# ScalarE's gate exponential and logarithm placed ahead of the four output-gate copies, in both layers of the second block

## The reference, cut to what matters

```
aq, ak, av, az, mq, mk, mv, mo, mz, mi, mf = project(xn, w_in)
q = rope_2d(aq); k = rope_2d(ak)
att_x = window_ctx_attention(q, k, v, kc, vc, sink) * silu(az)
...
lf = log_sigmoid(mf + b_f)        # per token and head, 2 directions
b  = cumsum(lf)                   # within chunks of 128 tokens
```

## Time and profile before

| | |
|---|---|
| median of three runs | 2201.64 us (2199.36 to 2202.74) |
| profiled execution: own time | 2193.12 us |
| profiled execution: span | 2191.3 us |
| mean granted TensorE clock | 0.98 |
| PE busy | 2060.9 us, 94% of the span |
| DVE busy | 775.5 us, 35% |
| ACT busy | 404.6 us, 18% |
| chain that ended last | PE 88%, DMA 4%, DVE 4%, ACT 2% |

### The profile page before, as it was taken

How to read it: one execution, slowest core, us unless ns; L and a number is a source line. 1 busy time by engine, 2 the same in 40 slices (tenths; PEclk the granted TensorE clock), 3 DMA queues, 4 the chain that set the end, 5 groups by cost and what they waited for, 6 DMA issues and landing times.

```text
span 2191.3 us, 36820 instructions
## 1 busy us (share of the span) xinstructions
PE 2060.9 (94%) x15880; PEld 1489.7 (68%) x15880; DVE 775.5 (35%) x1750; ACT 404.6 (18%) x958; POOL 5.8 (0%) x12
## 2 busy tenths in 40 slices
PE   7999999999989999999999999999999989899877
PEld 6869999886866666666666655567545675466766
DVE  5735655586231121111011111013256364235354
ACT  1232210104220111000100000002133422123221
POOL 0000000000000000000000000000000000000000
PEclk9979999999999999999999999999999999999998
DMA  8473444336189999999999999991211101222100
GB/s 306 172 247 119 171 176 173 135 136 248 39 328 370 420 418 417 420 421 420 420 419 420 421 420 418 418 416 81 97 57 39 40 38 58 76 98 77 58 20 19
DMA packets 71939, 506.73 MB, mean 231 GB/s; under 512 B 7776, under 2 KB 9824, under 8 KB 11232
## 3 DMA queue, kind: packets, MB, share of 16 engines
q1 hardware_dynamic: 69296, 497.18, 56.8%
q0 software_dynamic: 1152, 4.19, 0.8%
q10 hardware_dynamic: 1328, 2.97, 0.4%
HBM read 503.27 MB, written 1.05 MB: 230 GB/s over the span
## 4 chain that ended last, share of the span: by engine, by line
PE 88%; DMA 4%; DVE 4%; ACT 2%; issue 1%; SPq 0%; DVEq 0%; ACTq 0%
PE ps L449 86%; DMA work<-weights 2%; DMA ring<-weights 2%; PE ps L1114 1%; PE ps L690 1%; PE ps L566 0%; DVE work L2527 0%; DMA par<-params 0%; DVE work L1885 0%; ACT work L1707 0%; DVE work L2484 0%; DVE work L2488 0%; DVE work L2485 0%; DVE work L2594 0%; PE ps L1215 0%
## 5 line engine op out<-in xcount | busy, mean ns | idle before, releaser
L449 PE MATMUL ps<-work 128*32 128x256 f32 (+8 forms) x5608 | 596.0, 385 | 30.5 <-DVE work L2527 11.3
L449 PE MATMUL ps<-work,ring 128*128 128x256 f32 (+2 forms) x2056 | 524.1, 410 | 12.0 <-DVE work L2409 6.0
L449 PEld LDWEIGHTS ps<-work 128*32 128x32 f32 (+3 forms) x5608 | 382.9, 139 | 196.6 <-issue 122.4
L449 PE MATMUL ps<-ring,work 128*32 128x256 f32 (+3 forms) x4824 | 471.9, 413 | 13.0 <-DMA ring<-weights 3.9
L449 PEld LDWEIGHTS ps<-work,ring 128*128 128x128 f32 x2056 | 356.2, 193 | 151.8 <-issue 115.8
L449 PEld LDWEIGHTS ps<-ring,work 128*32 128x32 f32 (+1 forms) x4824 | 260.2, 120 | 150.8 <-issue 80.0
L449 PE MATMUL ps<-xc,ring 128*128 128x256 f32 (+1 forms) x1440 | 277.2, 354 | 11.1 <-DVE xc L1901 7.1
L449 PEld LDWEIGHTS ps<-xc,ring 128*128 128x128 f32 x1440 | 244.6, 193 | 45.2 <-issue 12.1
L2147 DVE TENSOR_TENSOR work<-work,ps 128x256 f32<-128x256 f32 x42 | 17.7, 421 | 419.4 <-ACT work L1564 419.4
L449 PE MATMUL ps<-xc,work 128*128 128x256 f32 (+1 forms) x720 | 138.3, 350 | 0.3 <-DMA work<-weights 0.3
L449 PEld LDWEIGHTS ps<-xc,work 128*128 128x128 f32 x720 | 120.8, 191 | 20.2 <-issue 3.8
(11 more groups left out here) (266 smaller groups left out, 1163.1 us busy)
## 6 DMA issues: line engine op xcount, KB each, us to landing
ring<-weights SPq DMA_DIRECT2D x317, 1024.0 KB, 12.0
work<-weights SPq DMA_DIRECT2D x154, 1024.0 KB, 16.0
work<-rel POOLq DMA_DIRECT2D x8, 512.0 KB, 11.1
con<-consts ACTq DMA_DIRECT2D x1, 1368.0 KB, 10.3
xc<-x_t SPq DMA_DIRECT2D x1, 1024.0 KB, 7.4
xc<-ctx_t ACTq DMA_DIRECT2D x1, 1024.0 KB, 21.5
out<-work SPq DMA_DIRECT2D x1, 1024.0 KB, 3.9
par<-params SPq DMA_DIRECT2D x1, 872.0 KB, 9.2
```

Source lines behind the costliest of these rows:

```text
L449: ins = eng.matmul(o, lhs, rhs, start=start, stop=stop, **kw)
```

## The change

In ScalarE's `block2_first` the wait for `lf_abs`, the exponential, the wait between the two, and the logarithm move from behind the four `Silu` copies of `az` to ahead of them. It holds for both layers. No instruction is added or removed and no other engine's program changes.

```
@@ -1647,13 +1647,13 @@
                     else:
                         n = 2 * T if l else T
                         eng.activation(ak[:, 0:n], o[:, 0:n], ACT.Copy).then_inc(s["aqk_copied"], 1)
-                for c in range(CC):
-                    o = tile(eng, "az", l, c)
-                    eng.activation(azs[:, c, 0:n_q], o[:, 0:n_q], ACT.Silu).then_inc(s["azs_out"], 1)
                 eng.wait_ge(s["lf_abs"], l + 1)
                 eng.activation(labs, labs, ACT.Exp, scale=-1.0).then_inc(s["lf_ln"], 1)
                 eng.wait_ge(s["lf_ln"], 2 * l + 1)
                 eng.activation(labs, labs, ACT.Ln, bias=con[:, CN("one")]).then_inc(s["lf_ln"], 1)
+                for c in range(CC):
+                    o = tile(eng, "az", l, c)
+                    eng.activation(azs[:, c, 0:n_q], o[:, 0:n_q], ACT.Silu).then_inc(s["azs_out"], 1)
```

## The result

The changed kernel has a median of 2180.73 us (2172.15 to 2183.27) against 2200.86 us (2199.36 to 2202.74) of the kernel before, four executions each: ratio 0.9908, 95% interval 0.9881 to 0.9934. That is 20.1 us less, where 12.4 us were forecast, and the time lies under the range of 2185 to 2196 us. The profiled execution took 2172.15 us with a span of 2170.3 us, 21.0 us less than the one of before.

A forecast was written before the change was run, and what follows sets the result against it. PE, busy 94% of the span, was taken to bound the kernel. Wait 8.11 plus clock 4.35 gave 12.46 us, less 0.1 for hand-offs 12.4, so 2201.64 - 12.4 = 2189.2 us, range 2185 to 2196.

The forecast's parts named there:

- Step 1, cover: ACT ahead of the `az` copies: loads, `Exp` and `Ln` are covered by PE's `az` matmuls, 1.1 us margin in layer 1, cost 0.
- Step 2, subtraction: DVE's subtraction behind `rope`: `lf` is ready some 9 us before PE's last `az` matmul ends in layer 1.
- Step 3, the wait: PE between `az` 3 and the prefix sums: idle goes, 4.16 + 3.95 = 8.11 us gained, residual 0 or a few hundredths.
- Step 4, table loads: ACT's table loads in each layer: four before and four after, the last ahead of the same instruction, cost 0.
- Step 5, the clock: PE from the prefix sums to the second scores: clock no longer falls, 2.77 us in layer 0, 1.58 in layer 1, together 4.35.
- Step 6, what is late next: DVE and ACT from first scores to first probabilities: still in time for PE, 0.6 us left in layer 0, 4 more in layer 1.
- The seams together: Both layers, from the end of `az` to the second scores: 8.11 us of wait plus 4.35 of clock, 12.46 us gained.
- The rival of the wait alone: Only the wait goes; the clock still falls there, or later losses eat its gain: 8.1 us gained, 2193.5 us, chance 0.23.
- the rival of one layer: Layer 1 gains nothing and only layer 0 gains: 6.9 us, 2194.7 us, chance 0.04.
- that of nothing: The DVE and ACT chains of the rounds bind the rest, so no gain arrives: 2201.6 us, chance 0.05.
- I take the same difference from the median: From profiled execution to median: the 12.4 us gain is also taken from the median 2201.64, giving 2189.2 us.
- a later fall that the shifted work now meets: Behind the two places, in the rival where only the wait goes: a later clock fall eats the clock's gain; chance 0.23.

The follow-up runs named there:

- before_late_start2: The kernel before with seven DVE memsets of 1024 scratch columns ahead of the first normalization, all work about 2 us later: mean 2203.8 us.

## Why the prediction was wrong

- **Step 1, cover:** right. The `Silu` load ended 2.36 us ahead of the first tile in layer 1, where 1.1 was worked out; the difference is the first table load, which runs ahead of the wait for `|f|`.
- **Step 2, subtraction:** right, directly behind `rope`.
- **Step 3, the wait:** right in the sum, with one miss: a residual of 0.19 us idle ahead of the first scores in layer 0 for the copy of `az` 3, where none was expected. The sums ended at 1571.71, the copy (1571.16 and 0.60 us) at 1571.76, and the scores started at 1571.90. The copy ended 0.05 us behind the sums instead of 0.1 ahead of them, and the hand-off of 0.14 us was left out. The layer still gained 6.84 us.
- **Step 4, table loads:** right, four loads before and after. The rule of the Trainium skill (page "ScalarE: Activation LUTs", section "Table sets: the hidden batching unit") that exponential and logarithm need one load again does not fit this kernel: the load between them is there at 1921.77.
- **Step 5, the clock:** right in mechanism, as PE kept busy shows in one trace, and in size: 4.35 us worked out, 4.4 in the changed kernel's trace and 4.3 with PE kept busy.
- **Step 6, what is late next:** right. The first turned probabilities (1581.19, and 1950.65 in layer 1) start without idle time.
- **The seams together:** 12.46 us worked out, 12.66 measured. The rival of the wait alone, the rival of one layer and that of nothing fell: both layers gain singly and together.
- **The step that failed** is the one from the seams to the median, "I take the same difference from the median", with the range hung on "the spread of the runs shown". Three executions within 3.4 us were taken for the kernel's spread. It is 27.6 us (2181.6 to 2209.2). The clues stood there: a profiled execution 8.5 us off the median, and the third slice of the page's clock line at 7 tenths in a stretch where PE is busy. Single executions scatter with a standard deviation of 5.6 us (before) and 6.8 us (changed), so the difference between two sets of four strays by some 4 to 5 us by chance (an estimate from these two), and the range had to hold that.
- **A term was missing** besides: the kernels are 17, not 12.4 us apart on average. The 4 us of clock outside the seams were not in the sum. They stood only in a rival, with the other sign ("a later fall that the shifted work now meets"), and as 1.6 us in the lower end of the range. Their cause stays open. Of the 20 us of the result, then, 12.7 are the seams, some 4 are clock elsewhere of unknown place, and the remaining 3 are within the chance of four executions.

## What to carry to other kernels

Put a small activation whose result starts the next stage ahead of the long queue of copies, if its input is early and a tile's matmuls cover its table loads; the last gap between copies is too short for it when loads and activations need 4.4 us and a tile 3.45. Read the gain at the seam in the trace, where it repeats to within some tenths of a us, and read the total at an equal mean clock; a few executions within 3 us of each other say nothing of a spread of 28. An idle time of PE that is removed may give clock back as well: at these two seams 2.7 us beside 4.2 and 1.7 beside 4.0, while a wait of 2.41 us cost no clock at all.

## What the hardware showed that was not expected

PE can be busy for all of 24.00 us and hold the clock of 1.2 GHz throughout (110 to 134 us of the kernel before), while the same work has 2.4 GHz in another execution; this one place moves the total by 10.9 us. Some 2 us ahead of it PE had stood idle for 0.99 us; the same 0.99 us stand in the changed kernel's trace (up to 109.83), and there the clock did not fall. After idle times of 0.50 and 0.63 us close together the clock fell for 3.4 us; after a single one of 2.41 us it did not, and after 2.62 us it fell. Nor does the wait alone set how long the fall lasts: the wait of layer 1 went with 3.4 us of low clock in the first trace of the kernel before and with 6.8 us in before_late_start2, the last 0.9 us of the wait among them. The table load is issued ahead of the wait of its activation in the gates (1913.59, 8 us early) but not ahead of the attention's first exponential (1942.01, behind the wait).
